# Rows of 264 instead of 256 elements in six activation buffers of a transformer block on Trainium2

## The reference, cut to what matters

```python
h = rms_norm(x, norm1_w)
proj = h @ w_in                        # 2048 x 6152
# four mLSTM heads and four differential attention heads of width 256 from proj
x = x + concat([hm, ha]) @ w_out       # 2048 x 2048
h = rms_norm(x, norm2_w)
x = x + (silu(h @ w_gate) * (h @ w_up)) @ w_down   # 2048 x 5632, 2048 x 5632, 5632 x 2048
```

## Time and profile before

| | us |
|---|---|
| median of 3 runs | 1163.6 |
| lowest, highest | 1162.82, 1163.88 |
| span of the profiled execution | 1158.5 |
| TensorE busy in it | 1142.4 |
| VectorE busy | 604.1 |
| ScalarE busy | 536.6 |

### The profile page before, as it was taken

The page is one execution under the profiler, slowest core; times in us unless marked ns, Lnnn a source line. Parts: engine busy times, 40 slices in busy tenths (PEclk is TensorE's granted clock), DMA queues, the critical chain, the costliest instruction groups (busy, mean ns, idle before and its releaser), DMA issues.

```text
span 1158.5 us, 14198 instructions
## 1 busy us (share of the span) xinstructions
PE 1142.4 (99%) x5128; PEld 939.2 (81%) x5128; DVE 604.1 (52%) x684; ACT 536.6 (46%) x659; POOL 10.9 (1%) x31
## 2 busy tenths in 40 slices
PE   7999999899999999999999999999999999999998
PEld 6888888688888888888888888888888888888886
DVE  6646555664565555554545554554544544454443
ACT  5645657654544454444434434444444433333332
POOL 3000000000000000000000000000000000000000
PEclk9989999999999999999999999999999999999999
DMA  8626545465465556666666666666666555555553
GB/s 255 204 90 208 175 128 162 128 217 154 140 206 174 183 180 200 183 199 183 181 199 187 191 189 189 185 196 182 186 194 187 185 191 184 191 186 186 192 186 127
DMA packets 98133, 210.37 MB, mean 182 GB/s; under 512 B 6856, under 2 KB 6928, under 8 KB 98096
## 3 DMA queue, kind: packets, MB, share of 16 engines
q1 hardware_dynamic: 97600, 209.74, 59.3%
q0 software_dynamic: 464, 0.11, 0.1%
q10 hardware_dynamic: 32, 0.01, 0.0%
HBM read 207.73 MB, written 2.10 MB: 181 GB/s over the span
## 4 chain that ended last, share of the span: by engine, by line
PE 96%; DVE 2%; ACT 1%; DMA 1%; issue 0%; SPq 0%; ACTq 0%
PE acc L389 27%; PE acc L391 27%; PE acc L392 27%; PE aux L391 4%; PE aux L389 4%; PE aux L392 4%; PE aux L403 2%; DVE w_lo L927 1%; DMA w_raw<-in_w_in 1%; DVE conv L1092 0%; PE aux L422 0%; PE aux L423 0%; PE aux L454 0%; ACT w_hi L669 0%; DVE res L1236 0%
## 5 line engine op out<-in xcount | busy, mean ns | idle before, releaser
L927 DVE TENSOR_TENSOR w_lo<-w_raw,w_hi 128x1024 fp32r<-128x1024 f32 x392 | 478.3, 1224 | 458.7 <-ACT w_hi L676 340.0
L676 ACT ACTIVATE w_hi<-w_raw 128x1024 fp32r<-128x1024 f32 x256 | 271.7, 1062 | 365.5 <-PE acc L392 227.0
L389 PE MATMUL acc<-w_lo,act_hi 128*128 128x512 f32 x1088 | 429.7, 395 | 4.1 <-DVE w_lo L927 3.9
L392 PE MATMUL acc<-w_hi,act_hi 128*128 128x512 f32 x1088 | 424.8, 390 | 0.0
L391 PE MATMUL acc<-w_hi,act_lo 128*128 128x512 f32 x1088 | 424.6, 390 | 0.0
L389 PEld LDWEIGHTS acc<-w_lo,act_hi 128*128 128x128 f32 x1088 | 205.1, 189 | 48.5 <-DVE w_lo L927 4.9
L392 PEld LDWEIGHTS acc<-w_hi,act_hi 128*128 128x128 f32 x1088 | 204.9, 188 | 43.2
L391 PEld LDWEIGHTS acc<-w_hi,act_lo 128*128 128x128 f32 x1088 | 205.3, 189 | 41.4
L669 ACT ACTIVATE w_hi<-w_raw 128x1024 fp32r<-128x1024 f32 x136 | 142.0, 1058 | 82.7 <-PE acc L392 69.8
L389 PE MATMUL acc<-w_lo,hid_hi 128*128 128x512 f32 x176 | 69.7, 396 | 0.0
L392 PE MATMUL acc<-w_hi,hid_hi 128*128 128x512 f32 x176 | 69.6, 396 | 0.0
(11 more groups left out here) (201 smaller groups left out, 570.2 us busy)
## 6 DMA issues: line engine op xcount, KB each, us to landing
w_raw<-in_w_in SPq DMA_DIRECT2D x96, 512.0 KB, 3.8
w_raw<-in_w_gate SPq DMA_DIRECT2D x88, 512.0 KB, 4.4
w_raw<-in_w_up SPq DMA_DIRECT2D x88, 512.0 KB, 3.8
w_raw<-in_w_down SPq DMA_DIRECT2D x88, 512.0 KB, 3.9
w_raw<-in_w_out SPq DMA_DIRECT2D x32, 512.0 KB, 4.4
res<-in_x SPq DMA_DIRECT2D x4, 512.0 KB, 8.5
out<-res SPq DMA_DIRECT2D x8, 256.0 KB, 3.6
w_if<-in_w_in POOLq DMA_DIRECT2D x1, 64.0 KB, 7.7
```

The source lines that it names most:

```text
L389: pe.matmul(bank[:], hi[:, k, tok], w_lo[:, slot, cols], start=first and kk == 0, stop=False)
L392: mm = pe.matmul(bank[:], hi[:, k, tok], w_hi[:, slot, cols], start=False, stop=last and kk == len(kts) - 1)
L676: act.activation(w_hi[:, c % SPLIT, :], w_raw[:, c % RAW, :], ACT.Copy).then_inc(hi_done, 1)
L927: dve.tensor_tensor(w_lo[:, slot, :], w_raw[:, slot, :], w_hi[:, slot, :].bitcast(F32), ALU.subtract).then_inc(lo_done, 1)
```

## The change

A row of each of the six buffers gets 264 elements (1056 bytes), of which the last 8 aren't used. A buffer of 24 floats (96 bytes), line_pad, is allocated ahead of the mixer's and feed-forward buffers. Where whole rows were addressed, the first 256 elements now are; the other accesses already name their tokens. Nothing else differs.

```diff
+ROW = SEQ + 8
...
-        act_hi = sb("act_hi", [KT, SEQ], F32R)
-        act_lo = sb("act_lo", [KT, SEQ], F32R)
+        act_hi = sb("act_hi", [KT, ROW], F32R)
+        act_lo = sb("act_lo", [KT, ROW], F32R)
...
+        sb("line_pad", [24])
+
         mix = ExitStack()
-        y_hi = sb("y_hi", [KT, SEQ], F32R, mix)
-        y_lo = sb("y_lo", [KT, SEQ], F32R, mix)
+        y_hi = sb("y_hi", [KT, ROW], F32R, mix)
+        y_lo = sb("y_lo", [KT, ROW], F32R, mix)
...
-        hid_hi = sb("hid_hi", [KF, SEQ], F32R, ff)
-        hid_lo = sb("hid_lo", [KF, SEQ], F32R, ff)
+        hid_hi = sb("hid_hi", [KF, ROW], F32R, ff)
+        hid_lo = sb("hid_lo", [KF, ROW], F32R, ff)
...
-                        act.activation(y_hi[:, 8 + 2 * h:10 + 2 * h, :],
+                        act.activation(y_hi[:, 8 + 2 * h:10 + 2 * h, 0:SEQ],
...
-                        dve.tensor_tensor(y_lo[:, ks, :], scaled[:, 0, :].rearrange("p (k s) -> p k s", k=2),
-                                          y_hi[:, ks, :].bitcast(F32), ALU.subtract).then_inc(y_lo_done, 1)
+                        dve.tensor_tensor(y_lo[:, ks, 0:SEQ], scaled[:, 0, :].rearrange("p (k s) -> p k s", k=2),
+                                          y_hi[:, ks, 0:SEQ].bitcast(F32), ALU.subtract).then_inc(y_lo_done, 1)
```

## The result

The changed kernel takes 1177.75 us, the median of four runs, against 1163.34 before: a ratio of 1.0133 (95% interval 1.0115 to 1.0151), 14.4 us slower. The forecast had the right sign, but 1171.4 and its upper end 1175.0 were too low.

A forecast was written before the change was run, and what follows sets the result against it. TensorE's matmul start distances were taken to bound the kernel. Act +12.2, y -1.1 and hid -3.3 us gave +7.8 on the 1163.6 us median: 1171.4 us, range 1168.0 to 1175.0, chance 0.80.

The forecast's parts named there:

- What bounds the kernel: Whole kernel: TensorE, busy 1142.4 of 1158.5 us; time is number of matmuls times distance between starts, waits hardly matter.
- Sign, and where it comes from: Whole kernel slower, chance 0.88: act matmuls lose 12.2 us, y gains 1.1 and hid 3.3, sum +7.8 us.
- 64 behaves like 0, and 96 like 32: Weight loads at offsets modulo 128: 0 and 64 cheap (226.7 ns per matmul), 32 and 96 dear, 6.7 ns more.
- The same step again in y and hid: y and hid matmuls: half their tiles become cheap, -4.8 us before changeover costs; with them y -1.1, hid -3.3 us.
- Changeovers: Switches between dear and cheap k tiles, every six matmuls in projections: 230.4 ns mean; total rises from +6.1 to +7.8 us.
- The base: Act matmuls before the change: 226.7 ns from start to start, from which 3264 x 3.75 ns = +12.2 us was reckoned.
- Only a multiple of 128 is cheap: Rival, chance 0.08: in all six buffers a steady run at offset 64 costs like 32; +14.8 us, 1178.4.
- Faster: Rival, chance 0.06: load-to-stream distance over 256 bytes or more counts; 1176 matmuls drop to 215 ns, net -10.2 us, 1153.4.
- Nothing: Rival, chance 0.06: the address plays no part, y and hid differ from act by their stages; time stays 1163.6.
- Clock, writes, moved buffers: Side terms: a half-clock stretch, up to 1.6 us either way; writes into wider rows, nothing; buffers moved behind y_lo, 0.04 us.

## Why the prediction was right or wrong

**What bounds the kernel: right.** The loss is in TensorE's distances of starts (15.7 of the 17.8 us between the spans, and 3.0 in the stretches at half clock); no wait, engine or queue adds to it. The wait in the earlier trace rows sums to 3.5 us in the profile after, 3.9 before.

**Sign, and where it comes from: right, for half a reason.** Act lay at the one best place, and wider rows take 14 of its 16 k tiles off it. That an address sets the distance of starts is shown by the run in which only the streams moved.

**The step that failed: "64 behaves like 0, and 96 like 32".** It took ten single loads, each behind a steady run at distance 0, for steady values. The trace of the kernel with rows of 272 shows that the first load at 64 leaves a short distance (0.22 us) and the next ones don't; held constant, 64 costs 233.3. It also counted the load's offset from a multiple of 128, where the runs show its distance from the stream modulo 256. With the right table half of the tiles aren't cheap; only those at 0, and those at 192 for the most part. The mean over the eight is 231.95 against the 230.0 I had before changeovers: 2.0 ns x 3264 = 6.4 us, the larger part of the error.

**The same step again in y and hid.** I let the pad put half of their tiles at cheap offsets. In the changed kernel y_hi, y_lo and hid_hi start at distance 128, hid_lo at 0 (the weights begin at 83072, 128 past a multiple of 256), and their rows too step through all eight distances. Their mean is then 231.95 before changeovers, not 230.0, against 233.3 before the change: they gained 1.8 us instead of 4.4.

**Changeovers: mis-sized, in act.** I had 230.4 - 230.0 = 0.4 ns per matmul, the runs show 232.6 - 231.95 = 0.65 ns: 2.1 us in all instead of 1.3. For the kernel with rows of 272 it is more: the mean of its four constants is (226.7 + 233.3 + 232.4 + 228.9)/4 = 230.3, it has 231.6. The cheap tiles bear it: in the changed kernel a k tile of act at distance 0 has 230.9 ns on the mean of its six. My rows for this had one changeover each between long steady runs. For that case they were read rightly: the kernel with half of act dear has 1.37 us for the six behind a dear run as well. What they couldn't show is a changeover every six matmuls.

**The base.** I took 226.7 ns for all of act before. It is 227.1, since the input projection, where other work comes between, has 227.7. That takes 1.4 us off the loss, and hides a part of the error above.

**The rivals.** "Only a multiple of 128 is cheap" was priced at 1178.4 and is close to 1177.75, but it is refuted: with the pad alone all buffers are at such a multiple, and y and hid stay at 232.4. Its figure is near because both readings make three quarters of the tiles dear. "Faster" had the right idea, the distance to the stream over a period of 256 bytes, and the wrong sign: no constant distance that was measured gives less than 226.7. "Nothing" fell with the run of moved streams. The Trainium skill's page TensorE: Matmul & The Clock Gate, section "Back-to-back issue gap", has about 216 ns for a single matmul of 512 columns by itself, and about 131 ns for a sustained stream of them. In fp32r no run here has less than 226.7 on the mean, at distance 0; only the plain fp32 matmuls of the earlier trace rows, with 256 columns, come to 215, and 131 is seen nowhere.

**Clock, writes, moved buffers.** Writes into wider rows and the moved mixer buffers cost nothing that shows (VectorE 604.6 us busy, ScalarE 535.8). The clock's allowance of 1.6 us was about right for one stretch; the profile after has a second one from 235 to 239 us.

**What stays open.** Which resource the load and the stream share, and why the distances settle at once behind some changeovers and not within six matmuls behind others. The runs show the distances, not the cause. Of the 1.3 us between the 15.7 us of the distances and the 14.4 us of the medians, 0.9 are the rest of the profiled executions; the low-clock stretches of the timed runs, which vary by some microseconds, would cover the 0.4 left, but that isn't shown.

## What to carry to other kernels

Where fp32r matmuls of 512 columns run back to back at full clock, put stationary and moving buffers at the same address modulo 256, and keep k tiles and slots at multiples of 256 bytes from each other, so that the distance never changes; 480 bytes of padding were worth 0.8% here. When a group's matmuls last some nanoseconds longer than another's with the same shape, compare addresses before anything else, and test with a pad. And don't read a steady cost from a single event that follows another state: read it from a long steady run, as the 24 distances here, and in the pattern in which the kernel will use it.

## What the runs showed of the hardware that I had not expected

- The distance of starts depends on the address of the loaded tile less that of the moving operand, modulo 256 bytes: 226.7 ns at 0, 228.9 at 192, 232.4 to 234.3 at the six other multiples of 32. Moving only the stream by 32 bytes took act from 226.8 to 233.3. The same distance gave the same value at different addresses: 192 in two runs (act, hid), 128 in two.
- It has a memory. One load in six at distance 32 costs some 11 ns beyond its own 6.7 in the matmuls behind it, 14 and 7 in turn; in runs of 48 the mean is that of the two constants (230.1 against 230.0).
- At half clock none of this shows: starts are 427 ns apart at distance 0, and just so in the changed kernel's second stretch (235.6 to 238.2 us, k tiles 4 and 5, distances 128 and 160).
